# The fourth tile of a stage is issued between the norm's sums and the norm's spread

## The reference

```
first_block: x = x + even_mixer(rmsnorm(x))        # windowed attention + pooling    ("ein" ... "eout")
             x = x + mlp(rmsnorm(x))               # 1024 -> 4096 -> 1024            ("up0", "down0")
             x = x + odd_mixer(rmsnorm(x))         # latent attention + recurrence   ("oin" ... "oout")
             x = x + mlp(rmsnorm(x))               #                                 ("up1", "down1")
             x = rmsnorm(x, final_norm)
second_block: u = rmsnorm(x, norm_mix) @ w_in      # 33 tiles of 128 columns         ("zin")
             h = x + concat(conv, sparse attention, dilated attention)(u) @ w_out    ("out2")
             h = h + sigmoid(h @ w_gate) * (p @ w_proj)                              ("ple")
             return rmsnorm(h, norm_final)
rmsnorm(x, g) = x * rsqrt(mean(x * x) + eps) * g
```

## Time and profile before

| what | value |
|---|---|
| median of three runs | 1613.89 us (1612.09 to 1614.36) |
| the profiled execution | 1611.82 us, its span 1610.0 us |
| mean granted TensorE clock | 0.969 |
| TensorE, VectorE, ScalarE, GpSimd busy | 93%, 49%, 39%, 35% |
| GpSimd's subtractions | 232, mean 2442 ns |
| TensorE's waits for a spread's reciprocal | L1460: 3.8 us in 6, L1463: 3.0 us in 1 |
| TensorE's waits for weights from GpSimd | 14.2 us in 8, the longest 4.3 |

### The profile page before, as it was taken

How to read it: one execution, slowest core, us unless ns; L and a number is a source line. 1 busy time by engine, 2 the same in 40 slices (tenths; PEclk the granted TensorE clock), 3 DMA queues, 4 the chain that set the end, 5 groups by cost and what they waited for, 6 DMA issues and landing times.

```text
span 1610.0 us, 20388 instructions
## 1 busy us (share of the span) xinstructions
PE 1489.6 (93%) x7110; PEld 1167.8 (73%) x7110; DVE 783.1 (49%) x1417; ACT 622.9 (39%) x1126; POOL 566.1 (35%) x236
## 2 busy tenths in 40 slices
PE   6979899999999987788999999999989799899997
PEld 5657678888888866545778888888867677666785
DVE  6783442223444677586333223444466236476434
ACT  4443332232323456545433232232353234655432
POOL 4222254444444433100235444444423352122441
PEclk9999999999999988979999999999989999899998
DMA  5212232322223221100123232332322232111221
GB/s 215 68 51 66 66 105 91 102 94 96 100 91 103 70 89 66 53 1 1 61 76 112 91 104 92 99 97 91 104 66 79 92 107 77 40 53 53 66 79 53
DMA packets 36624, 129.55 MB, mean 80 GB/s; under 512 B 4048, under 2 KB 4176, under 8 KB 36560
## 3 DMA queue, kind: packets, MB, share of 16 engines
q1 hardware_dynamic: 35136, 124.80, 23.7%
q10 hardware_dynamic: 1424, 3.90, 0.7%
HBM read 126.58 MB, written 2.10 MB: 80 GB/s over the span
## 4 chain that ended last, share of the span: by engine, by line
issue 58%; POOL 22%; PE 16%; DVE 2%; ACT 1%; POOLq 1%; DVEq 0%; ACTq 0%
POOL w L558 22%; PE bank L575 4%; PE bank L577 4%; PE bank L576 4%; PE bank L698 1%; PE bank L712 1%; PE bank L680 1%; DVE arena L1996 0%; POOLq L557 0%; POOLq L555 0%; ACT tmp L1114 0%; ACT tmp L1104 0%; DVE arena L1628 0%; DVE arena L1886 0%; ACT arena L1383 0%
## 5 line engine op out<-in xcount | busy, mean ns | idle before, releaser
L558 POOL TENSOR_TENSOR w<-raw,w 128x1024 fp32r<-128x1024 f32 x232 | 565.9, 2442 | 1010.8 <-ACT w L1048 628.2
L575 PE MATMUL bank<-opC,w 128*128 128x512 f32 x624 | 255.3, 409 | 26.0 <-POOL w L558 14.2
L577 PE MATMUL bank<-opC,w 128*128 128x512 f32 x624 | 246.8, 395 | 0.0
L576 PE MATMUL bank<-opC,w 128*128 128x512 f32 x624 | 246.4, 395 | 0.0
L1604 DVE TENSOR_TENSOR mlp_op<-arena,mlp_op 128x512 fp32r<-128x512 f32 x64 | 144.5, 2260 | 188.7 <-ACT mlp_op L1171 188.7
L575 PE MATMUL bank<-mlp_op,w 128*128 128x512 f32 x560 | 221.5, 396 | 10.0 <-DVE arena L1516 9.5
L1143 ACT ACTIVATE w<-raw 128x1024 fp32r<-128x1024 f32 x126 | 133.2, 1057 | 239.5 <-PE bank L577 239.5
L576 PE MATMUL bank<-mlp_op,w 128*128 128x512 f32 x560 | 220.5, 394 | 0.0
L577 PE MATMUL bank<-mlp_op,w 128*128 128x512 f32 x560 | 220.3, 393 | 0.0
L575 PE MATMUL bank<-opA,w 128*128 128x512 f32 x428 | 168.8, 394 | 6.8 <-ACT arena L1317 2.3
L577 PE MATMUL bank<-opA,w 128*128 128x512 f32 x428 | 167.4, 391 | 0.0
(11 more groups left out here) (213 smaller groups left out, 1928.2 us busy)
## 6 DMA issues: line engine op xcount, KB each, us to landing
raw<-stream_dram SPq DMA_DIRECT2D x232, 512.0 KB, 3.4
out_t_dram<-arena SPq DMA_DIRECT2D x8, 256.0 KB, 2.1
x<-x_t_dram SPq DMA_DIRECT2D x4, 256.0 KB, 5.7
x<-x_t_dram ACTq DMA_DIRECT2D x4, 256.0 KB, 7.2
rope<-ropes_dram ACTq DMA_DIRECT2D x2, 512.0 KB, 6.8
con<-consts_dram ACTq DMA_DIRECT2D x1, 993.5 KB, 8.2
arena<-p_t_dram ACTq DMA_DIRECT2D x1, 512.0 KB, 4.2
par<-params_dram ACTq DMA_DIRECT2D x1, 253.5 KB, 3.8
```

Of the source, the lines that this page charges most:

```text
L558: pool.tensor_tensor(w_lo[:, j, :], raw[:, j, :], w_hi[:, j, :].bitcast(F32), ALU.subtract).then_inc(lo_made, 1)
L575: pe.matmul(out, wh, hi, start=first, stop=False)
L576: pe.matmul(out, wh, lo, start=False, stop=False)
L577: return pe.matmul(out, wl, hi, start=False, stop=last)
```

## The change

In `head`, the fourth tile is issued behind `norm_sums`; what stood between (the spread, in `ein` the two rotations, in `zin` both spreads) is handed in as `between` and run ahead of a given product of that tile: the spread ahead of the third product, in `zin` the spreads ahead of the second and the sixth. In `zin` the tile moves from bank 6 to bank 5. The filling work of `last` begins with the fifth tile, and eight steps (28 to 35) take three products in place of four. The asides keep their places relative to the tiles, but for `turn27`. On VectorE the logarithms of step 13 move ahead of the step's evictions; the fourth tile is evicted, and its code added, ahead of the attention. ScalarE prepares one more block ahead of it.

```diff
-Z_ASIDES = {3: ((4, "turn27"),), 7: ((4, "turn28"),), 10: ((4, "turn29"),), 11: ((4, "hid0"),), 14: ((4, "hid1"),),
+Z_ASIDES = {4: ((1, "turn27"),), 7: ((4, "turn28"),), 10: ((4, "turn29"),), 11: ((4, "hid0"),), 14: ((4, "hid1"),),
@@ pace @@
-    return 4 if step < 36 else 3
+    return 4 if step < 28 else 3
@@ z_steps @@
-    work = [w for w in z_work(HEAD)] + [("out2", i, k) for i, k in OUT2_HEAD]
-    done, blocks, at, ends = [], [], 0, HEAD
+    work = [w for w in z_work(HEAD + 1)] + [("out2", i, k) for i, k in OUT2_HEAD]
+    done, blocks, at, ends = [], [], 0, HEAD + 1
@@ head, TensorE @@
-            def head(stage, op, norm, after_down=False):
+            def head(stage, op, norm, between, after_down=False):
...
                 norm_sums(norm)
+                t = t0 + HEAD
+                if t >= 4:
+                    pe.wait_ge(z_ready, t - 3)
+                pe.wait_ge(lo_made, b0 + HEAD + 1)
+                for k in range(KT):
+                    if k in between:
+                        between[k]()
+                    mm = product(bank[4 + t % 4][:, :], (b0 + HEAD) % RING, k, *splits[op, k], k == 0, k == KT - 1)
+                mm.then_inc(acc_full, 1)
@@ the five calls @@
-                head(f"up{layer}", op, op)
-                norm_spread(op)
-                for j in range(HEAD, RING):
-                    up(0, j)
+                head(f"up{layer}", op, op, {2: lambda: norm_spread(op)})
-            for k in range(E_AHEAD):
-                if k in (2, 5):
-                    rotate_even(k // 3)
-                e_product("ein", HEAD, k)
+            head("ein", "even", "even", {2: lambda: norm_spread("even"), 5: lambda: rotate_even(0), 7: lambda: rotate_even(1)})
-            head("oin", "odd", "odd", after_down=True)
-            norm_spread("odd")
-            linear("oin", split_operand("odd"), headed=HEAD)
+            head("oin", "odd", "odd", {2: lambda: norm_spread("odd")}, after_down=True)
+            linear("oin", split_operand("odd"), headed=HEAD + 1)
-            head("zin", "mix2", "final", after_down=True)
-            norm_spread("final")
-            norm_spread("mix2")
+            head("zin", "mix2", "final", {1: lambda: norm_spread("final"), 5: lambda: norm_spread("mix2")}, after_down=True)
@@ beside_last, TensorE @@
+                if step == TURN_LAG - 1:
+                    pe.wait_ge(z_ready, z_tile(Z_HOSTS[HEAD]) + 1)
@@ ScalarE @@
-                if step >= 1:
-                    for name in Z_DONE[step - 1]:
-                        after_zin(name)
+                for name in Z_DONE[step - 1] if step else Z_HOSTS[:HEAD + 1]:
+                    after_zin(name)
-            prepare(block0 + HEAD + RING - 1)
+            prepare(block0 + HEAD + RING)
@@ behind_last, VectorE @@
-                for name in Z_DONE[s]:
-                    evict(name)
-                    after_evict(name)
                 if s == DILATED // 2 + 1:
                     dve.wait_ge(log_den, 1)
...
+                for name in Z_DONE[s]:
+                    evict(name)
+                    after_evict(name)
...
-            for name in Z_HOSTS[:HEAD]:
+            for name in Z_HOSTS[:HEAD + 1]:
                 evict(name)
+                after_evict(name)
```

More of the change, by code:

```diff
@@ L446, in z_banks @@
                 held[4 + (t0 + n) % 4] = z_tile(Z_HOSTS[n])
-            for n in range(HEAD, len(Z_HOSTS)):
+            out[Z_HOSTS[HEAD]] = (4 + (t0 + HEAD) % 4, None)
+            held[4 + (t0 + HEAD) % 4] = z_tile(Z_HOSTS[HEAD])
+            for n in range(HEAD + 1, len(Z_HOSTS)):
                 own, other = 6 + (n + 1) % 2, 6 + n % 2
@@ L767, in mlp @@
                     down(FF // P // RING - 1, j, False, j == RING - 1)
-            head("ein", "even", "even")
-            norm_spread("even")
             def rotate_even(n):
@@ L975, in z_fill @@
             def z_fill():
-                for kind, n, what in z_work(HEAD):
+                for kind, n, what in z_work(HEAD + 1):
                     if kind == "aside":
```

## The result

The changed kernel takes 1625.1 us (median of 6 runs, 1622.4 to 1630.0); the kernel before, in runs beside them, 1614.1 (1612.1 to 1617.4). The ratio is 1.0065, 95% interval [1.0049, 1.0081]: 10.5 us slower, where +3.9 was forecast. The direction was right. The time is 1.1 us above the upper end of the range.

The account below looks back on a forecast made before the run. TensorE, busy 93% of the span, was taken as the bound, with VectorE chains behind the heads' gaps. Terms 0.8 - 2.3 - 5.4 + 3.8 + 4.4 + 2.6 = +3.9 us gave 1617.8 on the median; range 1610 to 1624.

Parts of the forecast that it names:

- `oin`: Norm of oin: the VectorE chain started 0.8 us later loses its slot behind GpSimd's subtraction; +0.8 us, bounds -0.5 and +0.8.
- `zin` to step 1: From zin's sums to the scores of attention step 1: 22.1 us becomes 19.8, so -2.3, with the low clock gone.
- Steps 28 to 35: Last attention: eight products fewer beside these steps, -5.4 us, from 4.95 read for seven.
- Waits for weights: Steps 2 to 7 of the last attention: TensorE's weight waits grow from 12.2 to 16.0 us, +3.8; bounds 0 and +6.
- The wait at step 13: Last attention: TensorE stands waiting for the logarithms that VectorE makes in its own step 13; +4.4 us, bounds 2.0 and 4.8.
- the fall behind it: After the step 13 wait the granted clock drops to half for a stretch: +2.6 us, with 0 as the other end.
- signs of being wrong: Step 13 wait under 3 us, weight waits at or under 12, or an up0 loop tile earlier than 9.5 us after the sums.
- 0 each: Norms of up0 and up1: the spread's 0.8 us delay disappears behind GpSimd's subtraction, the loop start stays; 0 us each.
- "0" for `ein`: Norm of ein: TensorE still waits for the second rotation, whose chain is VectorE's, so the delay costs 0 us.
- rival 3: In up0, up1 or ein a norm misses its slot, 2.4 us each; one or two make +6.3 to +8.7; chance 0.14.
- Rivals 1 and 2: At step 13: 1, clock stays up, +1.3 us, chance 0.24; 2, wait is short, -1.1 or -4.9, chance 0.09.
- Rival 4: The change does nothing of note in the attention, only the heads' gaps close: about -10 us, 1604; chance 0.05.

Follow-up runs that it names:

- `zin` alone: The kernel before with the change in zin and the last attention only, the other heads as before: 1.0021, +3.4 us.
- the four heads: The kernel before with the change in up0, up1, ein and oin only, zin and the last attention as before: 1.0064, +10.3 us.
- repaired `zin`: The kernel before with the change in zin and the last attention, but step 0 gives up the eight products instead of steps 28 to 35: 0.9974, -4.2 us.

## Why the prediction was wrong, step by step

**What bounds the kernel** was read rightly, and so were the chains. `up0`, `up1` and `ein`: the 0.8 us delay disappeared in the slot behind GpSimd's subtraction, and the loop tile came at an unchanged distance from the sums. `oin`: forecast a wait 1.3 longer, measured 1.07, and +0.8 us in the run where it is alone. `zin` to step 1: -2.4, forecast -2.3. Steps 28 to 35: -5.5, forecast -5.4 (its own rows, 4.95 us for seven, make 5.7 for eight). Waits for weights: +2.2, forecast +3.8. The wait at step 13: 4.07, forecast 4.4; the fall behind it about 3.0 us (8.0 for the step, less 4.07 and the 0.9 of the spread that moved into it), forecast 2.6. That half was forecast at +3.1 and measured at +3.4, and part of this agreement is luck. The waits grew by less than forecast, but steps 2 to 12, from the scores of step 2 to those of step 13, took 5.4 us more in the profile with `zin` alone (112.8 before, 118.2). Only 2.2 of it are waits; the other 3.2 are the same 498 matmuls at a lower clock (TensorE busy 99.6, then 102.7). The prediction's sum had nothing for that. None of its signs of being wrong came (the 9.48 us at `up0` are the 9.49 of before), because none of them looked at the clock behind the heads.

**The step that failed is "0 each" for `up0` and `up1` and the "0" for `ein`.** Measured alone, it is `up1`'s 0 that is clear of noise: +6.9. The working saw that each head's idle time (0.6 us, at `ein` 1.1) would be joined to the wait behind it, "now some 2 us" at `up0` and `up1`, and priced that at nothing because the end of the wait did not move. In the sum a new fall of the clock was weighed at one place only, step 13 (rival 3 had one in steps 6 or 7). There the prediction took from single rows (full clock behind 2.49 and 3.16 us, half clock behind 4.26) that such short waits leave the clock alone. The seventeen profiles, gathered, say otherwise. Behind `up1`'s wait the clock fell in all 5 profiles in which it is 2.0 us and idle, and in none of 6 in which it is 1.3 us and idle. Behind `up0`'s 2.0 us it fell in 1 of 5. Behind `ein`'s it fell in all 4 profiles with 3.3 us, and in 4 of 9 with 2.2. The very rows that the prediction leaned on vary too. Eleven profiles have the last attention in the order of the kernel before. In them the clock fell behind the same 2.5 us wait of step 4 six times, and behind the 3.2 us wait of step 5 six times. The 4.5 us behind these two waits, in the kernel before and then with `oin` alone:

```profile
1248.69:1253.19 4.50, 4.50 (x20) 3.74 (x21) 0.40 (x1) 0.00 (x0) 2.67 (x1) 1.00 0.52 142
1260.12:1264.62 4.50, 4.50 (x22) 3.75 (x23) 0.69 (x1) 0.00 (x0) 2.29 (x1) 1.00 0.52 164
```
```profile
1249.09:1253.59 4.50, 4.50 (x13) 3.63 (x14) 0.40 (x1) 0.00 (x0) 2.62 (x1) 0.63 0.43 151
1262.12:1266.62 4.50, 4.50 (x13) 3.52 (x14) 0.00 (x0) 0.00 (x0) 2.26 (x1) 0.62 0.57 174
```

One profile is one draw: a row with full clock behind a wait does not show that the wait is safe.

The Trainium skill (TensorE: Matmul & The Clock Gate, Part 1) says that a monitor throttles the clock when TensorE has been idle and that activity releases it. The runs with matmuls in the waits agree: 10.3 us of the four heads became 0.3. The prediction cited that page for the gain at `zin` and the loss at step 13, and did not take it to the lengthened waits behind the heads.

**The size.** The prediction's terms for the four heads make +0.8; they cost +10.3. A fall at `up1` is worth 1.6 us at the place. One at `ein` is worth 1.6 in two of the profiles with the 3.3 us wait and 2.6 and 2.9 in the other two, and the 2.2 us wait of before had it already in four of nine. The rest of `up1`'s 6.9 lies far behind it, and delaying the program by 1.3 us at full clock makes 3.9. **What stays open:** alone, `ein`, the two `up` heads and `oin` cost -0.3, 5.0 and 0.8, together 5.5 (interval some 2 to 9) against 10.3 (8.1 to 12.6). With `up0` and `up1` taken apart (0.6 and 6.9) the sum is 8.0 (some 4 to 12), which does not differ from 10.3. Whether the heads add is open. Nor is it shown why `up1` costs more than its one fall, and `ein` and `up0` do not.

**The rivals.** Rivals 1 and 2 needed a clock that stays up, or a short wait, at step 13; neither came. Rival 3 was nearest in size, +6.3 to +8.7, with the wrong mechanism: no norm missed its slot. Rival 4, the gaps closing for -10, did not happen. The repaired `zin` shows what was right in it: the tile gains there once the fill is put back in step.

## What to carry to other kernels

Idle time joined to idle time is not free, even when the end of the wait stays put. Here no idle wait of 1.3 us at `up1` was followed by a fall of the clock, and waits of 2.0 to 3.3 us were in some executions: price such a lengthened wait with a fall, at a chance and not at yes or no. When a tile moves ahead of a loop with work dealt out in steps, take its work from the first step, so that every later step keeps what it had (here worth 7.6 us). Where TensorE must wait, matmuls without a use, fewer than the wait holds, kept its clock here; the filling of the longest waits (5.8 us) and a few shorter ones gained 5.8 us.

## What the runs showed of the hardware that was not expected

- The granted clock falls at different waits in different executions of one order. From 84 to 95 us, ahead of which and in which most of them have the same order, the kernel before and one other show a granted clock of 1.00, the fifteen others 0.69 to 0.84. The kernel before ranged from 1611.6 to 1620.9 us over its runs, 0.6%.
- Its profiled execution, 1611.8 us, lay 2 to 5 us under its medians. A sum made against one profile carries that difference.
- Matmuls in a wait cost nothing that shows: 24 of them took 5.6 us, a wait of 0.5 was left, and the tile behind it ran at full clock.
- VectorE's two-input multiplication, started 0.7 us later beside the same GpSimd subtraction, took 1.59 us instead of 2.27.
